# The exponents of seven products of an HGRN2 layer formed on GpSimd instead of VectorE

## The chip, the cores and the metric

One core of a Trainium2 chip runs the whole program. The time is the device time of one execution in microseconds (us). Each engine (TensorE, VectorE, ScalarE, GpSimd, SyncE) works through its own list of instructions in order and waits on semaphores for the others. In the profile TensorE is PE (its weight loads PEld), VectorE is DVE, ScalarE is ACT, GpSimd is POOL and SyncE is SP.

## What is computed

The reference is one step of a two-layer decoder: a retention layer with a dense SwiGLU, then an HGRN2 layer with a top-2-of-8 expert SwiGLU, for one prompt of 256 tokens and 8 single sample tokens. The change touches the HGRN2 layer's recurrence, cut here to what matters:

```python
q = silu(q); forget = lb + (1 - lb) * sigmoid(f)        # 8 heads of 128
k = 1 - forget; logf = log(forget)
# chunks of 64 tokens; b is the running sum of logf in a chunk
b = cumsum(logf)
w = exp(where(t >= s, b[t] - b[s], -inf))
a[t, s] = sum_d q[t, d] * w[t, s, d] * k[s, d]
o = a @ i + (q * exp(b)) @ S
S_new = S * exp(b_last) + (k * exp(b_last - b)).T @ i
```

The sample tokens need one step each: the state of a head (8 samples x 128 x 128) is read from memory, decayed, given its rank-one term and written back.

## The kernel before, in words

The decay between two tokens depends on the channel, so the products of q and k are made level by level. At level l the tokens are cut into groups of 2m (m = 2^l); the later half carries q times exp(b - middle), the earlier half k times exp(middle - b), and one matrix product then gives the pairs of that group. There are ten products, p = 0 to 9: p 0 is the diagonal, p 1 the weighted k for the final state (transposes), p 2 crosses the two blocks of 128 tokens, and p 3 to 9 are the levels 0 to 6.

The stage runs over sixteen tiles t (a projection of 128 output columns each, `HG_TILE`: eight of i, eight of the gate g). `HG_STEP` = (0, 1, 2, 3, 5, 6, 8, 9, 10, 11) says after which tile TensorE makes product p. Product p uses the work array `lev[p % 2]`, and makes four passes over engines before TensorE can begin:

- **exponents(p)** (L1550 to L1580, VectorE): waits until TensorE has finished product p - 2, which read the same array, and writes the differences of the running sums `bcum` into `lev[p % 2]`: for the levels 0 to 5 two subtractions of 128x1024 (L1564, L1565), for level 6 two of 128x512 and two copies (L1568, L1569). It raises `lev_sub`.
- **exponential(p)** (L1085, ScalarE): waits on `lev_sub` and takes exp of the whole array in place (L1088).
- **operands(p)** (L1582, VectorE): two multiplications by q and k (L1592, L1593), then raises `lev_x` for TensorE.
- after the product, **choose** (VectorE, L1599) or **take** (ScalarE, L1090) moves the results out of the banks.

The order of the work in one tile t is written out by hand for each engine:

- VectorE (L1649): choose of the product after tile t - 1; exponents for the product after tile t + 1; scaled(t), which reads the tile out of its bank (L1312); the low part of the weights four tiles ahead (`low_part`, L1317), which waits for ScalarE's high part of the same weights; update_head(t - 1) (L1613, L1620), eight instructions on the samples' state; operands for the product after tile t + 1.
- ScalarE (L1122): take; exponential of the same product; the copies of `itr` (L1133, L1135); the high part of the weights four tiles ahead (L965); the decay of head t's state (L1145).
- TensorE (L2207): the tile; `rows_of_i` (L2107), which waits for update_head(t - 2) and for scaled(t - 1); `spread_i`; the product. A tile goes into bank t % 2, which ScalarE's itr copy has to free.
- GpSimd (L888 to L894): it issues the transfers of the samples' state. Three buffers (`hunit`) are filled ahead; then for h = 0 to 7 it waits for update_head(h), issues the store of head h, waits for the store's end and issues the load of head h + 3. After that it issues the router's weights and three rows of gains (L896 to L903).

So the tiles 2, 4, 5, 7, 8, 9 and 10 form exponents, for the products 3 to 9. The stage's tail follows without exponents, then the output projection, the router and the eight experts, whose weights come from memory one piece after another (SyncE, L788).

Of the kernel before, what the change touches and what calls it, by code (L numbers as in the profile page):

```python
# [7 lines left out]
ALU = mybir.AluOpType  # L8
# [7 lines left out]
P = 128  # L16
# [7 lines left out]
HH = 8  # L24
# [6 lines left out]
CHUNK = 64  # L31
# [126 lines left out]
HG_LEVEL = (None, 8, 7, 0, 1, 2, 3, 4, 5, 6)  # L158
HG_TILE = [("hi", i) for i in range(8)] + [("hg", i) for i in range(8)]
HUNITS = 3  # L160


def products_after(t):

    return [p for p in range(len(HG_STEP)) if HG_STEP[p] == t]
# [111 lines left out]
def hybrid_step(nc, ins, outs):  # L277
    FILL, BANKS = fills()
    with ExitStack() as ctx:
# [63 lines left out]
        def part(tensor, a, *shape):  # L343
            n = int(np.prod(shape))
            v = tensor[:, a:a + n]
            if len(shape) == 2:
                return v.rearrange("p (a b) -> p a b", a=shape[0])
            if len(shape) == 3:
                return v.rearrange("p (a b c) -> p a b c", a=shape[0], b=shape[1])
            return v  # L350
# [60 lines left out]
        bcum = part(arena, 8448, 8, NP_)  # L411
# [3 lines left out]
        lev = [part(ring, scratch + 2048 * j, 2048) for j in range(2)]  # L415
        hs_out = part(ring, scratch, 8, P)

        hunit = [part(ring, a, NS, P) for a in (scratch + 4096, scratch + 5120, spare)]
# [4 lines left out]
        std8 = arena[0:8, 13568:13568 + NT]  # L423
        rstd8 = arena[0:8, 13568 + NT:13568 + 2 * NT]
        oH = hk
        fsmp = part(small, 64, 8, 8)
        tots = part(small, 128, 4, 8)

# [122 lines left out]
        lev_sub = sem("level_exponents")  # L551
# [5 lines left out]
        hu_out = [sem(f"hunit_stored{j}") for j in range(HUNITS)]  # L557
# [36 lines left out]
        def filled(eng, name):  # L594

            b, k = FILL[name]
            eng.wait_ge(bank_full[b], k + 1)
# [5 lines left out]
        def freed(eng, name):  # L603

            b, k = FILL[name]
            eng.wait_ge(bank_free[b], k + 1)
# [240 lines left out]
        @block.gpsimd  # L847
        def _(pool):
            nc.gpsimd.memset(ring[:, spare:spare + 1024], 0.0).then_inc(pad_zero, 1)

            def load_state(u):
                b, h = unit_of(u)
                j = u % UNITS
                if u >= UNITS:
                    pool.wait_ge(unit_out[j], 16 * (u // UNITS))
                pool.dma_start(unit[:, j, :].rearrange("p (k e) -> p k e", k=2), ret_in[b, h])\
                    .then_inc(unit_s[j], 16)

            pool.wait_ge(arrived[0], need[dense[0][0]])
            for u in range(UNITS):  # L860
                load_state(u)
            for p_ in range(PAIRS):
                for u in (2 * p_, 2 * p_ + 1):
                    b, h = unit_of(u)
                    freed(pool, ("vb", u))
                    pool.dma_start(ret_out[b, h], unit[:, u % UNITS, :].rearrange("p (k e) -> p k e", k=2))\
                        .then_inc(unit_out[u % UNITS], 16)
                for u in (2 * p_ + 4, 2 * p_ + 5):
                    if UNITS <= u < NS * RH:
                        load_state(u)  # L870

            for h in range(UNITS):
                pool.wait_ge(unit_out[h], 16 * len(range(h, NS * RH, UNITS)))
            pool.wait_ge(s_store, 16 * RH)
            filled(pool, ("sot", RH - 1))
            nc.gpsimd.memset(zeros, 0.0).then_inc(zero_ok, 1)
            pool.wait_ge(zero_ok, 1)
            nz = YROWS // P
            pool.dma_start(y_scr[:, :].rearrange("(t p) d -> p t d", p=P),
                           zeros.to_broadcast([P, nz, D])).then_inc(zero_stored, 16)  # L880

            def load_h(h):
                if h >= HUNITS:
                    pool.wait_ge(hu_out[h % HUNITS], 16 * (h // HUNITS))
                    filled(pool, ("itr", h - HUNITS + 1))
                pool.dma_start(hunit[h % HUNITS], hg_in[h]).then_inc(hu_in[h % HUNITS], 16)

            for h in range(HUNITS):  # L888
                load_h(h)
            for h in range(HH):  # L890
                freed(pool, ("ib", 1, h))
                pool.dma_start(hg_out[h], hunit[h % HUNITS]).then_inc(hu_out[h % HUNITS], 16)
                if h + HUNITS < HH:
                    load_h(h + HUNITS)  # L894

            pool.dma_start(w_rt, ins["moe_router"][0].rearrange("(k p) e -> p k e", p=P)).then_inc(rt_in, 16)  # L896
            pool.dma_start(gfin, ins["final_norm_g"].partition_broadcast(P)).then_inc(rows_in, 16)
            freed(pool, ("lv", 4, 3))
            pool.dma_start(g_row, ins["norm_ffn_g"][1].partition_broadcast(P)).then_inc(rows_in, 16)
            filled(pool, ("hvar", 0))  # L900
            for c in range(4):
                pool.dma_start(g_group[32 * c:32 * c + 32, 0, :],
                               ins["norm_ffn_g"][1][256 * c:256 * c + 256].partition_broadcast(32)).then_inc(rows_in, 16)  # L903
            pool.wait_ge(h_tok_ok, 3)
            pool.wait_ge(rows_ok, 1)
            pool.wait_ge(xe_ok, 1)
            for t in range(3):
                m = P if t < 2 else NS
                for w in range(2):
                    pool.indirect_dma_start(y_scr[:, :], bass.IndirectOffsetOnAxis(ap=rowi[0:m, w, t:t + 1], axis=0),  # L910
                                            h_tok[0:m, t, :], None).then_inc(x_scattered, 16)

            pool.wait_ge(w_seen, 32)
            for t in (2, 0, 1):
                m = P if t < 2 else NS
                for w, dst in enumerate((ya, yb)):
                    pool.indirect_dma_start(dst[0:m, t, :], None, y_scr[:, :],
                                            bass.IndirectOffsetOnAxis(ap=rowi[0:m, w, t:t + 1], axis=0))\
                        .then_inc(ya_in[t], 16)
# [333 lines left out]
        def _(dve):  # L1253
# [280 lines left out]
                    forget(h - 1)  # L1534
            forget(HH - 1)

            bch = bcum.rearrange("p h (c t) -> p h c t", t=CHUNK)
            T = [bch[:, :, c, CHUNK - 1] for c in range(4)]

            def sums():  # L1540
# [9 lines left out]
            def exponents(p):  # L1550

                l = HG_LEVEL[p]
                if p >= 3:
                    filled(dve, (("kt", 3), ("cr", 1))[p - 3] if p < 5 else ("lv", p - 4, 3))
                L = lev[p % 2]
                lc = L.rearrange("p (h c t) -> p h c t", h=8, t=CHUNK)
                tot = lambda a, b: bch[:, :, a:b, CHUNK - 1:CHUNK].to_broadcast([P, 8, b - a, CHUNK])
                if l <= 5:
                    m = 1 << l
                    n = 2048 // (2 * m)  # L1560
                    bv = bcum.rearrange("p h t -> p (h t)").rearrange("p (n t) -> p n t", t=2 * m)
                    lv = L.rearrange("p (n t) -> p n t", t=2 * m)
                    mid = bv[:, :, m - 1:m].to_broadcast([P, n, m])
                    V.tensor_tensor(lv[:, :, m:], bv[:, :, m:], mid, ALU.subtract)  # L1564
                    i = V.tensor_tensor(lv[:, :, 0:m], mid, bv[:, :, 0:m], ALU.subtract)  # L1565
                elif l == 6:
                    for c in (0, 2):
                        V.tensor_tensor(lc[:, :, c:c + 1, :], tot(c, c + 1), bch[:, :, c:c + 1, :], ALU.subtract)  # L1568
                        i = V.tensor_copy(lc[:, :, c + 1, :], bch[:, :, c + 1, :])  # L1569
                elif l == 7:  # L1570
                    link(V.tensor_tensor(lc[:, :, 0:2, :], tot(0, 2), bch[:, :, 0:2, :], ALU.subtract))
                    V.tensor_tensor(lc[:, :, 0, :], lc[:, :, 0, :], tot(1, 2)[:, :, 0, :], ALU.add)
                    V.tensor_copy(lc[:, :, 2, :], bch[:, :, 2, :])
                    i = V.tensor_tensor(lc[:, :, 3, :], bch[:, :, 3, :], tot(2, 3)[:, :, 0, :], ALU.add)
                else:
                    link(V.tensor_tensor(lc, tot(0, 4), bch, ALU.subtract))
                    for c in range(3):
                        i = V.tensor_tensor(lc[:, :, c, :], lc[:, :, c, :],
                                            tots[:, c, :].unsqueeze(2).to_broadcast([P, 8, CHUNK]), ALU.add)
                i.then_inc(lev_sub, 1)  # L1580
# [68 lines left out]
            for t in range(16):  # L1649
                for p in products_after(t - 1):  # L1650
                    if p == 0 or 3 <= p <= 6:
                        choose(max(p - 2, 0))
                for p in products_after(t + 1):
                    if p >= 3:
                        exponents(p)
                kind, i = HG_TILE[t]
                if kind == "hi" and i >= 2:
                    filled(dve, ("ib", 1, i - 2))
# [720 lines left out]
```

## Time and profile before

| | |
|---|---|
| median of 3 runs | 1653.11 us (1652.49 to 1654.35) |
| profiled execution, span of its instructions | 1650.9 us |
| PE busy, share of the span | 1605.4 us, 97% |
| DVE busy | 621.5 us, 38% |
| ACT busy | 421.5 us, 26% |
| POOL busy | 79.3 us, 5% |
| mean granted TensorE clock | 0.982 of full speed |

A row of the timeline gives the start and the duration in us, the engine, the line, the operation with the tile it writes and those it reads, the form and the number of instructions merged; in brackets stands how long the engine had been idle and what released it. The parts of the chain of waits are read in the same way. The profile's own execution gives the durations; the time of a run is some 2 us more than its span.

### The profile page before, as it was taken

The page shows a single profiled execution, that of the slowest core. Times are in us where ns is not written, and L with a number is a line of the kernel's source. Part 1 is how long each engine was busy: PE and PEld are TensorE (multiplying, and loading weights), DVE is VectorE, ACT ScalarE, POOL GpSimd, SP SyncE. Part 2 cuts the span into 40 slices and gives each one's busy share as a digit, 9 for nine tenths or more (in the row PEclk, how much of TensorE's full clock was granted, in tenths as well). Part 3 has the DMA queues.
Part 4 walks back from the last instruction along what each step waited for, and adds up shares of the span by engine and source line. Part 5 has one row for each costly group of instructions (what it writes and reads, how often), then busy time and mean ns, then how long its engine had stood idle before and what let it go on. Part 6 is the DMA issues. An engine that isn't in the chain of part 4 may idle for free.

```text
span 1650.9 us, 32102 instructions
## 1 busy us (share of the span) xinstructions
PE 1605.4 (97%) x14348; PEld 956.0 (58%) x14348; DVE 621.5 (38%) x934; ACT 421.5 (26%) x606; POOL 79.3 (5%) x106
## 2 busy tenths in 40 slices
PE   7999999999999988999999999999999999999997
PEld 7888877999999988884333333333333333333332
DVE  6666677566656787454010011100101101001114
ACT  4444544444455564632001000000010000100101
POOL 1122221000000011001000000000000000000001
PEclk9999999999999999997999999999999999999999
DMA  9678779455455443356999999999999999999995
GB/s 338 219 268 300 287 258 385 161 170 188 146 186 195 164 140 124 96 227 264 400 412 397 413 417 391 423 418 388 420 401 405 417 386 424 416 392 420 404 408 211
DMA packets 138232, 514.93 MB, mean 312 GB/s; under 512 B 6700, under 2 KB 61172, under 8 KB 129780
## 3 DMA queue, kind: packets, MB, share of 16 engines
q1 hardware_dynamic: 117780, 447.93, 70.1%
q0 software_dynamic: 15824, 57.97, 10.0%
q10 hardware_dynamic: 4496, 7.02, 1.3%
q8 instruction: 113, 1.85, 0.5%
q14 instruction: 19, 0.16, 0.0%
HBM read 472.43 MB, written 40.47 MB: 311 GB/s over the span
## 4 chain that ended last, share of the span: by engine, by line
PE 82%; DVE 8%; issue 2%; DMA 2%; ACT 1%; SPq 0%; POOL 0%; DVEq 0%; ACTq 0%
PE ps L1879 80%; DMA ring<-in_moe_w_down 2%; DVE ring_low_parts L1317 1%; DVE ring L1620 1%; ACT ring_low_parts L965 1%; DVE ring L1366 1%; PE ps L2025 1%; DMA ring<-in_state_retention 1%; DVE arena L1610 1%; DVE ring L1593 0%; DVE ring L1592 0%; DVE ring L1565 0%; DVE arena L1544 0%; DVE ring L1564 0%; DVE expert_arena L1846 0%
## 5 line engine op out<-in xcount | busy, mean ns | idle before, releaser
L1879 PE MATMUL ps<-ring,expert_x_turned 128*32 128x448 f32 x5376 | 508.1, 539 | 0.0
L1879 PEld LDWEIGHTS ps<-ring,expert_x_turned 128*32 128x32 f32 x5376 | 174.5, 110 | 330.9 <-issue 330.9
L1879 PE MATMUL ps<-normed_high,ring_low_parts 128*128 128x264 f32 x1344 | 271.2, 293 | 10.8 <-DVE arena L1312 3.0
L1879 PE MATMUL ps<-ring,expert_hidden_turned 128*32 128x512 f32 x2496 | 269.3, 592 | 0.2 <-DMA ring<-in_moe_w_down 0.2
L1317 DVE TENSOR_TENSOR ring_low_parts<-ring,ring_low_parts 128x1024 fp32r<-128x1024 f32 (+2 forms) x180 | 208.0, 1163 | 97.1 <-ACT ring_low_parts L965 97.0
L965 ACT CAST ring_low_parts<-ring 128x1024 fp32r<-128x1024 f32 (+2 forms) x180 | 180.0, 1001 | 244.4 <-PE ps L1879 240.1
L1879 PEld LDWEIGHTS ps<-normed_high,ring_low_parts 128*128 128x128 f32 x1344 | 220.3, 193 | 13.4 <-ACT arena L1135 3.6
L1811 DVE TENSOR_TENSOR expert_arena<-expert_arena,ps 128x1344 f32<-128x1344 f32 x16 | 24.9, 1554 | 507.2 <-PE ps L1879 507.2
L1879 PEld LDWEIGHTS ps<-ring,expert_hidden_turned 128*32 128x32 f32 x2496 | 81.0, 110 | 186.3 <-issue 184.2
L1879 PE MATMUL ps<-normed_low,ring_low_parts 128*128 128x264 f32 x640 | 163.9, 290 | 0.0
L1879 PE MATMUL ps<-h_parts,ring_low_parts 128*128 128x264 f32 x1056 | 130.0, 285 | 0.2 <-DVE h_parts L1301 0.2
L1879 PEld LDWEIGHTS ps<-h_parts,ring_low_parts 128*128 128x128 f32 x1056 | 129.2, 188 | 0.9 <-DVE h_parts L1301 0.4
L1879 PEld LDWEIGHTS ps<-normed_low,ring_low_parts 128*128 128x128 f32 x640 | 124.3, 194 | 0.3 <-issue 0.2
L1229 ACT ACTIVATE expert_arena<-ps 128x1344 f32<-128x1344 f32 x16 | 20.7, 1291 | 383.6 <-PE ps L1879 383.6
L1220 ACT COPY cst<-ps 32x1536 f32<-32x1536 f32 x16 | 22.9, 1432 | 370.3 <-PE ps L1879 370.1
L1806 DVE TENSOR_TENSOR cst<-ps,cst 32x1536 f32<-32x1536 f32 x16 | 28.0, 1751 | 223.7 <-ACT cst L1220 222.9
L1879 PE MATMUL ps<-mixed_high,ring_low_parts 128*128 128x264 f32 x384 | 76.0, 295 | 1.7 <-DVE normed_high L1684 0.9
L1879 PE MATMUL ps<-expert_piece_slot,expert_x_turned 128*32 128x448 f32 x768 | 75.1, 539 | 0.3 <-DMA expert_piece_slot<-in_moe_w_up 0.3
L1879 PEld LDWEIGHTS ps<-mixed_high,ring_low_parts 128*128 128x128 f32 x384 | 62.2, 194 | 4.7 <-issue 3.4
L1879 PE MATMUL ps<-hidden_high,ring_low_parts 128*128 128x264 f32 x352 | 64.2, 284 | 0.0
L1879 PE MATMUL ps<-ring 128*128 128x128 f32 (+1 forms) x368 | 52.1, 414 | 5.8 <-DVE ring L1593 2.4
L1879 PEld LDWEIGHTS ps<-hidden_high,ring_low_parts 128*128 128x128 f32 x352 | 54.6, 188 | 0.0
(285 smaller groups left out, 1231.3 us busy)
## 6 DMA issues: line engine op xcount, KB each, us to landing
ring<-in_moe_w_gate SPq DMA_DIRECT2D x64, 1792.0 KB, 16.7
ring<-in_moe_w_down SPq DMA_DIRECT2D x48, 2048.0 KB, 21.3
ring<-in_moe_w_up SPq DMA_DIRECT2D x48, 1792.0 KB, 18.4
expert_piece_slot<-in_moe_w_up SPq DMA_DIRECT2D x16, 1792.0 KB, 19.1
ring<-in_ret_w_in SPq DMA_DIRECT2D x8, 2048.0 KB, 12.9
ring<-in_state_retention POOLq DMA_DIRECT2D x32, 512.0 KB, 8.0
out_ret_s<-ring POOLq DMA_DIRECT2D x32, 512.0 KB, 4.8
ring<-in_hg_w_in SPq DMA_DIRECT2D x8, 2048.0 KB, 8.2
```

The costliest lines, as they stand in the source:

```text
L965: A.copy(block_hi(n), block_raw(n)).then_inc(fw_hi_ok, 1)
L1220: A.copy(y_out[64 * q:64 * q + 32], ps[64 * q + 32:64 * q + 64, b:b + TG, :]).then_inc(y_half_ok, 1)
L1229: A.activation(act_g, ps[:, b:b + TG, 0:GW], ACT.Silu).then_inc(gate_ok, 1)
L1317: V.tensor_tensor(block_lo(n), block_raw(n), block_hi(n).bitcast(F32), ALU.subtract).then_inc(fw_lo_ok, 1)
L1366: i = V.scalar_tensor_tensor(out=S, in0=bank(("vb", u)), scalar=ksmp[:, 2 * h + k, b:b + 1], in1=S, op0=ALU.mult, op1=ALU.add)
L1610: i = V.copy_predicated(dst, lvl[:, l - 1, :].unsqueeze(1).to_broadcast([P, 4, P]), src)
L1620: i = V.scalar_tensor_tensor(out=S[:, b, :], in0=bank(("ib", z, h))[:, P * (b % 4):P * (b % 4) + P], scalar=hk[:, h, NP_ + b:NP_ + b + 1], ...
L1806: V.tensor_tensor(y_out[z], ps[z, b:b + TG, :], y_out[z], ALU.add).then_inc(y_ok, 1)
L1811: V.tensor_tensor(act_g, act_g, ps[:, b:b + TG, 0:GW], ALU.mult).then_inc(mult_ok, 1)
L1879: return nc.tensor.matmul(out, lhsT, rhs, start=first, stop=last)
L2025: i = nc.tensor.transpose(bank(("vb", u))[:, P * e:P * e + P], col, ident)
```

## The change

VectorE's `exponents` keeps only the products 1 and 2. The same differences for the products 3 to 9 are formed by a new function of the same name in GpSimd's list, with the same waits for the product that last read the array, and the same signal `lev_sub`. GpSimd's loop over heads becomes a loop over tiles: in tile t it forms the exponents of the product that follows tile t + 1, then issues the load of head t + 1 (for heads 3 to 7), then the store of head t - 1. Before the loop it waits until VectorE's two remaining exponents are done. ScalarE's, TensorE's and SyncE's lists are unchanged, as is the rest of VectorE's.

```diff
+            def exponents(p):
+                G = nc.gpsimd
+                l = HG_LEVEL[p]
+                filled(pool, (("kt", 3), ("cr", 1))[p - 3] if p < 5 else ("lv", p - 4, 3))
+                L = lev[p % 2]
+                if l <= 5:
...
+                    G.tensor_tensor(lv[:, :, m:], bv[:, :, m:], mid, ALU.subtract)
+                    i = G.tensor_tensor(lv[:, :, 0:m], mid, bv[:, :, 0:m], ALU.subtract)
+                else:
...
+                    for c in (0, 2):
+                        total = bch[:, :, c:c + 1, CHUNK - 1:CHUNK].to_broadcast([P, 8, 1, CHUNK])
+                        G.tensor_tensor(lc[:, :, c:c + 1, :], total, bch[:, :, c:c + 1, :], ALU.subtract)
+                        i = G.tensor_copy(lc[:, :, c + 1, :], bch[:, :, c + 1, :])
+                i.then_inc(lev_sub, 1)
             for h in range(HUNITS):
                 load_h(h)
-            for h in range(HH):
-                freed(pool, ("ib", 1, h))
-                pool.dma_start(hg_out[h], hunit[h % HUNITS]).then_inc(hu_out[h % HUNITS], 16)
-                if h + HUNITS < HH:
-                    load_h(h + HUNITS)
+            pool.wait_ge(lev_sub, 2)
+            for t in range(16):
+                for p in products_after(t + 1):
+                    if p >= 3:
+                        exponents(p)
+                if HUNITS <= t + 1 < HH:
+                    load_h(t + 1)
+                if 1 <= t <= HH:
+                    freed(pool, ("ib", 1, t - 1))
+                    pool.dma_start(hg_out[t - 1], hunit[(t - 1) % HUNITS]).then_inc(hu_out[(t - 1) % HUNITS], 16)
...
 @block.vector, in the loop over t
-                for p in products_after(t + 1):
-                    if p >= 3:
-                        exponents(p)
```

## Rows read from the trace of the kernel before

**Rows 1.** Busy time by stage: window, length, then each engine's busy time, clock, DMA
```profile
577.00:679.00 102.00, 90.84 (x700) 88.00 (x698) 81.41 (x140) 56.36 (x131) 13.50 (x16) 0.92 0.40 122
679.00:708.00 29.00, 28.98 (x227) 26.33 (x228) 10.98 (x17) 16.88 (x26) 2.02 (x4) 1.00 0.27 95
790.00:1618.00 828.00, 827.47 (x8446) 274.67 (x8442) 102.47 (x57) 40.90 (x31) 0.00 (x0) 1.00 1.01 407
```

**Rows 2.** Who waited for whom, 577 to 679: total us, times, longest us
```profile
ACT ring L1088 <- DVE ring L1565: 37.6, 6, 10.3
...
DVE ring_low_parts L1317 <- ACT ring_low_parts L965: 20.6, 8, 2.9
```

**Rows 3.** Timeline of DVE through tile 5
```profile
617.73 1.22 DVE L1564 TENSOR_TENSOR ring<-arena 128x1024 f32<-128x1024 f32 x1
618.86 1.22 DVE L1565 TENSOR_TENSOR ring<-arena 128x1024 f32<-128x1024 f32 x1
...
623.33 1.23 DVE L1317 TENSOR_TENSOR ring_low_parts<-ring,ring_low_parts 128x1024 fp32r<-128x1024 f32 x1 [2.91 <-ACT ring_low_parts L965]
624.48 2.15 DVE L1620 SCALAR_TENSOR_TENSOR ring<-ps,arena,ring 128x128 f32<-128x128 f32 x8
```

**Rows 4.** Timeline of ACT: the exponentials, one cast and one take
```profile
591.00 1.91 ACT L1088 ACTIVATE ring<-ring 128x2048 f32<-128x2048 f32 x1 [3.19 <-DVE ring L1565]
...
609.03 1.91 ACT L1088 ACTIVATE ring<-ring 128x2048 f32<-128x2048 f32 x1 [5.75 <-DVE ring L1565]
...
620.11 1.91 ACT L1088 ACTIVATE ring<-ring 128x2048 f32<-128x2048 f32 x1 [5.56 <-DVE ring L1565]
...
622.24 1.06 ACT L965 CAST ring_low_parts<-ring 128x1024 fp32r<-128x1024 f32 x1
...
639.65 1.91 ACT L1088 ACTIVATE ring<-ring 128x2048 f32<-128x2048 f32 x1 [7.26 <-DVE ring L1565]
...
650.73 1.91 ACT L1088 ACTIVATE ring<-ring 128x2048 f32<-128x2048 f32 x1 [5.56 <-DVE ring L1565]
...
664.23 1.91 ACT L1088 ACTIVATE ring<-ring 128x2048 f32<-128x2048 f32 x1 [10.31 <-DVE ring L1565]
...
667.04 3.47 ACT L1111 COPY arena<-ps 16x64 f32<-16x64 f32 x16
```

**Rows 5.** Timeline of POOL: its compute instructions and what follows one
```profile
0.26 0.10 POOL L2370 MEMSET const-float32-0.0<- 128x1 f32 x1 [0.26 <-issue]
...
247.62 0.95 POOL L876 MEMSET ring<- 128x1024 f32 x1 [3.91 <-DMA out_ret_s<-ring]
248.87 1.31 POOL L879 DMA_DIRECT2D y_scr<-ring  x1 [0.30 <-POOL ring L876]
```

**Rows 6.** Timeline of POOL: issues of the head states, stores and one load
```profile
589.00 0.89 POOL L892 DMA_DIRECT2D out_hg_s<-ring  x1 [336.19 <-DVE ring L1620]
...
597.81 0.89 POOL L892 DMA_DIRECT2D out_hg_s<-ring  x1 [3.83 <-DVE ring L1620]
606.19 0.88 POOL L886 DMA_DIRECT2D ring<-in_state_hgrn  x1 [7.49 <-DMA out_hg_s<-ring]
...
616.04 0.89 POOL L892 DMA_DIRECT2D out_hg_s<-ring  x1 [2.56 <-DVE ring L1620]
...
635.32 0.89 POOL L892 DMA_DIRECT2D out_hg_s<-ring  x1 [2.98 <-DVE ring L1620]
646.47 0.89 POOL L892 DMA_DIRECT2D out_hg_s<-ring  x1 [10.26 <-DVE ring L1620]
657.87 0.89 POOL L892 DMA_DIRECT2D out_hg_s<-ring  x1 [10.51 <-DVE ring L1620]
```

**Rows 7.** Timeline of PE: tile 5 after a gap, the products 8 and 9
```profile
611.32 0.39 PE L1879 MATMUL ps<-normed_high,ring_low_parts 128*128 128x264 f32 x1 [1.53 <-ACT arena L1135]
...
670.73 3.84 PE L1879 MATMUL ps<-ring 128*128 128x128 f32 x32 [0.87 <-DVE ring L1593]
...
679.02 3.84 PE L1879 MATMUL ps<-ring 128*128 128x128 f32 x32 [1.54 <-DVE ring L1593]
```

More of the change, by code:

```diff
@@ L425, in hybrid_step @@
         oH = hk
+        bch = bcum.rearrange("p h (c t) -> p h c t", t=CHUNK)
         fsmp = part(small, 64, 8, 8)
@@ L886, in load_h @@
                 pool.dma_start(hunit[h % HUNITS], hg_in[h]).then_inc(hu_in[h % HUNITS], 16)
+            def exponents(p):
[4 more added lines that the diff above has]
+                if l <= 5:
+                    m = 1 << l
+                    n = 2048 // (2 * m)
+                    bv = bcum.rearrange("p h t -> p (h t)").rearrange("p (n t) -> p n t", t=2 * m)
+                    lv = L.rearrange("p (n t) -> p n t", t=2 * m)
+                    mid = bv[:, :, m - 1:m].to_broadcast([P, n, m])
+                    G.tensor_tensor(lv[:, :, m:], bv[:, :, m:], mid, ALU.subtract)
+                    i = G.tensor_tensor(lv[:, :, 0:m], mid, bv[:, :, 0:m], ALU.subtract)
+                else:
+                    lc = L.rearrange("p (h c t) -> p h c t", h=8, t=CHUNK)
+                    for c in (0, 2):
[3 more added lines that the diff above has]
+                i.then_inc(lev_sub, 1)
             for h in range(HUNITS):
                 load_h(h)
-            for h in range(HH):
-                freed(pool, ("ib", 1, h))
-                pool.dma_start(hg_out[h], hunit[h % HUNITS]).then_inc(hu_out[h % HUNITS], 16)
-                if h + HUNITS < HH:
-                    load_h(h + HUNITS)
+            pool.wait_ge(lev_sub, 2)
[8 more added lines that the diff above has]
+                    pool.dma_start(hg_out[t - 1], hunit[(t - 1) % HUNITS]).then_inc(hu_out[(t - 1) % HUNITS], 16)
             pool.dma_start(w_rt, ins["moe_router"][0].rearrange("(k p) e -> p k e", p=P)).then_inc(rt_in, 16)
@@ L1535, in _ @@
             forget(HH - 1)
-            bch = bcum.rearrange("p h (c t) -> p h c t", t=CHUNK)
             T = [bch[:, :, c, CHUNK - 1] for c in range(4)]
@@ L1552, in exponents @@
                 l = HG_LEVEL[p]
-                if p >= 3:
-                    filled(dve, (("kt", 3), ("cr", 1))[p - 3] if p < 5 else ("lv", p - 4, 3))
                 L = lev[p % 2]
@@ L1557, in exponents @@
                 tot = lambda a, b: bch[:, :, a:b, CHUNK - 1:CHUNK].to_broadcast([P, 8, b - a, CHUNK])
[L1558 to L1570, printed above, removed]
+                if l == 7:
                     link(V.tensor_tensor(lc[:, :, 0:2, :], tot(0, 2), bch[:, :, 0:2, :], ALU.subtract))
@@ L1652, in _ @@
                         choose(max(p - 2, 0))
-                for p in products_after(t + 1):
-                    if p >= 3:
-                        exponents(p)
                 kind, i = HG_TILE[t]
```

## The prediction, made before the change was run

> **What bounds the kernel now.** I read the busy time by stage first, then the waits of the stage that the change touches, then the timeline of each of its engines. Over the whole span PE is the busiest, and in the expert part it is busy 827.47 of 828 us beside a saturated memory [rows 1]. Nothing of the change reaches that far, so only a shift of its start can come through. The stage of the levels, 577 to 679, is different: PE shows 90.84 of 102 us with a granted clock of 0.92, DVE 81.41, ACT 56.36, POOL 13.50 [rows 1]. No engine is full; the time is set by a loop that goes from engine to engine. From 679 to 708 PE is full again (28.98 of 29) [rows 1]. So what the stage gains or loses by 679 goes to the end one to one.
>
> The loop is seen in tile 5 [rows 3, 4]. DVE forms exponents from 617.73 to 620.09; ACT, idle for 5.56 us, starts the exponential at 620.11; behind it in ACT's list stand the itr copies and the cast of weights, which starts at 622.24. DVE's low part waits for that cast, idle for 2.91 us, and starts at 623.33; the update of the head follows at 624.48 and ends near 626.5. Then come the operands, and the next tile's exponents. The two waits of that kind sum to 37.6 us of ACT (6 times) and 20.6 us of DVE (8 times) [rows 2]. The reader is to see that **the exponents are on this loop, and that DVE is idle right after them**: a busy engine's work is not saved if the loop still has to wait for the same result.
>
> **The change part by part.**
>
> *What DVE loses.* Six levels of two instructions, each taking its engine 1.13 us from start to start (617.73 to 618.86) [rows 3], and a seventh level, about 1.9: some 15.5 us. In tiles 2, 4, 5, 7, 8, 9 and 10 DVE then comes to the low part earlier and waits there for ACT's cast, which waits behind the exponential. This is a gain only if the exponents come earlier than before.
>
> *What POOL's instruction costs.* The trace has no two-input instruction on POOL. The nearest rows are a memset of the same width, 0.95 us, and one of a single column, 0.10 [rows 5]: 0.85 for one pass over 1024 columns. A subtraction makes three passes, two reads and a write. If all overlap it takes 0.95, if the reads are in series 1.8, if nothing overlaps 2.65 (2.85 with three whole memsets). I take 2.2, the middle of 1.8 and 2.65, since one engine serving three streams is nearer to these than to a fill. From a memset's end to what waited for it on the same queue lie 0.30 us [rows 5]; I add it once a level for ACT's start, against 0.02 from DVE. So a level costs 2 x 2.2 + 0.3 = **4.7 us**, DVE's 2.27; bounds 1.9 and 5.7. Strided blocks of one and two columns (levels 0 and 1) might cost POOL more; no row shows it.
>
> The Trainium skill (GPSIMD Engine Reference, § 3.1) gives 4497 ns for a subtraction-like instruction of 2048 fp32 on GpSimd and 2293 on VectorE. An estimate from that page is 2.25 for each of ours, 4.8 a level, and the sum below would become about 0.6 us larger.
>
> *Where it stands in POOL's queue.* In tile t the exponents stand behind the store of head t - 2, which waits for update_head(t - 2), done by DVE in its tile t - 1. The store's issue takes 0.89 [rows 6] and begins some 0.4 after the update. So they aren't formed as soon as the array is free: they begin 1.3 us after the update, where DVE began after its operands (2.27, in the tiles that have them) and its choose (2.45, likewise). "A level ahead" is at most that lead. Tile by tile, with the shift carried on from store to store [rows 6] and compared with the start of ACT's exponential [rows 4]:
>
> - p 3, tile 2 (before: neither operands nor choose between): 589.00 + 0.89 + 4.7 = 594.6 against 591.00, **+3.6**.
> - p 4, tile 4: the queue also holds the load of head 4, which waits for the end of the store of head 1. That store is issued at 597.81 and its end releases the load at 606.19, 8.4 later, as it runs beside a weight piece of 2 MB. Now: 597.81 + 3.6 = 601.4, + 8.4 = 609.8, load 0.88, store of head 2 0.89, exponents 4.7 = 616.3 against 609.03, **+7.3**. Without the slow transfer it would be + 4.6.
> - p 5, tile 5: 616.04 + 7.3 + 0.89 + 4.7 = 628.9 against 620.11, **+8.8**.
> - p 6, tile 7: 635.32 + 8.8 + 5.6 = 649.7 against 639.65, **+10.1**.
> - p 7, tile 8: 646.47 + 10.1 + 5.6 = 662.2 against 650.73, **+11.5**.
> - p 8, tile 9: 657.87 + 11.5 + 5.6 = 675.0 against 664.23, **+10.8**: here DVE had both operands and choose in front, and POOL wins 0.7.
> - p 9, tile 10: POOL has no store in front and is done near 678.6. ACT first does the exponential of p 8 and the cast (3.2 from 675.0, by 620.11 to 622.24 + 1.06) and the take, 3.47 [rows 4], to 681.7. Exponential (1.9), cast (1.0), low part (1.2) and operands (2.3) follow, ready near 688.1. But PE starts product 8 at 670.73 + 10.8 = 681.5 and needs it and tile 11, 6.75 us (670.73 to 679.02 less the gap of 1.54) [rows 7], so it reaches product 9 at 688.2 and finds it ready; before it was 679.02. **+9.2** at the entry of the full stretch.
>
> *Clock.* After the gap of 1.53 us before tile 5 [rows 7] the matmuls show 0.42 us instead of 0.28, and the stage's mean is 0.92, which is 16 us in 102 at the 1.2 GHz level. The gaps of PE in front of tiles 3, 5, 6, 8 and 9 become some 3 to 5 us long, since the tile's bank is freed by ACT behind the exponential. PE has slack in these very tiles, so I put this at +1, bounds 0 and +3.
>
> *The moved loads.* Each load of heads 3 to 7 is still behind the store that frees its buffer, and now behind the exponents too. ACT's decay of such a head comes after an exponential that waits for the same queue, so the transfer runs beside that wait: 0, bounds 0 and +2. The router's and gain rows' issues come 20 us later, and are needed after 715: 0. POOL's wait for DVE's first two exponents ends before 572: 0.
>
> **Sum.** 9.2 + 1 = +10.2 us on a profiled span of 1650.9, so 1661.1; the median of the runs is 1653.1, some 2.2 above the span, and the forecast for it is **1663.2**.
>
> The sum falls or rises by about 1.25 us for each 0.1 us of POOL's instruction (two to a level, on the loop a little over six times). With 1.8 it is +5, with 2.85 +18.
>
> **The rivals.**
>
> *Faster.* If POOL took less than about 1.4 us for a 128x1024 subtraction, a level would be below what DVE's operands, choose and exponents took together in tiles 5, 7, 8 and 9, and the loop would shorten; at 0.95, the memset's price, the sum is 10.2 - 1.25 x 12.5 = -5, or 1648. For it speaks only that this is the one compute row of POOL at that width; against it that a memset reads nothing. Point of decision: 1.4 us.
>
> *POOL and DVE block each other.* The Trainium skill (SBUF, § Who interferes with whom) says that a VectorE instruction with two SBUF inputs and a GpSimd instruction that reads SBUF exclude each other, the later one waiting for the whole of the earlier. No row of before can show it. As a mechanism here: in tiles 5, 8 and 9 POOL is ready 1.3 us after the update, while DVE's operands (two SBUF inputs) run for 2.27, so POOL waits 1.0 each time, and in tile 10 its last pieces collide with the low part and the operands of product 8 for another 0.5. Sum +3.5 on the forecast, 1666.7.
>
> *POOL is dearer than three passes.* With the small blocks of the low levels at 3.3 us an instruction, a level costs 6.9; 1.1 x 12.5 = +14 on the forecast, about 1677.
>
> *It does not show.* The chain is shorter than worked out (POOL at 1.6, no slow store): within 3.3 us of before.
>
> **How the numbers follow.** Chances: forecast with POOL between 1.8 and 2.7 us and no blocking 0.45; with blocking 0.25; dearer POOL 0.13; no difference 0.09; faster 0.08. The forecast's own range is 1658 to 1670. For 8 in 10 I take 1656.5 to 1674, which leaves out the faster case, most of the same one and half of the dearer one. A measurement of this kernel tells some 0.2% (3.3 us) from no change; slower by more 0.82, within 0.10, faster by more 0.08.
>
> **What would show it.** In the profile after: POOL's L-lines of the subtractions at 2.2 us; ACT's waits for the exponential released by POOL instead of DVE, and growing from the 37.6 us of its six longest to over 50; DVE's wait for the cast growing from 2.9 to between 5 and 8 us in those tiles, with its busy time down by 15.5; PE's gaps in front of tiles 3, 5, 6, 8, 9; the full stretch starting near 688 and everything behind it shifted alike. The steps go wrong if POOL's instruction is short, if the store of head 1 ends early (then -2.7), or if ACT's exponential starts at 594.6, 616, 629, 650, 662 and 675 in no such order.

## The result and the profile after

The changed kernel takes **1661.38 us** (median of 4 runs, 1658.44 to 1664.01) beside 1652.8 us for the kernel before in the same comparison: a ratio of 1.0056, with a 95% interval of 1.004 to 1.0071. It is slower by about 9 us. The prediction was 1663.2 us in a range of 1656.5 to 1674.

| | before | after |
|---|---|---|
| span of the profiled execution | 1650.9 us | 1662.2 us |
| DVE busy | 621.5 us | 608.6 us |
| POOL busy | 79.3 us | 111.2 us |
| stage of the levels (see below) | 112.05 us | 123.60 us |
| from there to the end | 965.3 us | 964.1 us |

The stage is measured from PE's product 0 to its head outputs, both of which stand in the timeline as one row. The two rows of each kernel, before first, then after:

```profile
573.57 3.81 PE L1879 MATMUL ps<-arena 128*128 128x128 f32 x32 [0.20 <-issue]
...
685.62 5.52 PE L1879 MATMUL ps<-arena 128*128 128x128 f32 x48
```

```profile
574.52 3.81 PE L1889 MATMUL ps<-arena 128*128 128x128 f32 x32 [1.75 <-issue]
...
698.12 5.52 PE L1889 MATMUL ps<-arena 128*128 128x128 f32 x48
```

685.62 - 573.57 = 112.05 and 698.12 - 574.52 = 123.60: +11.55 us in the stage. After has 0.95 more in front of it and 1.2 less behind it, which makes the span's 11.3. So the loss is in this stage, and it goes to the end one to one.

The busy time of these two windows, before and then after (columns as in rows 1):

```profile
573.57:685.62 112.05, 100.87 (x785) 98.03 (x786) 83.70 (x142) 63.32 (x139) 13.50 (x16) 0.92 0.45 142
```

```profile
574.52:698.12 123.60, 106.06 (x785) 102.97 (x786) 70.66 (x126) 63.13 (x139) 45.19 (x32) 0.89 0.39 121
```

DVE does 13 us less, in a stage that is 11.5 us longer. Its freed time has become waiting. The waits of after from 577 to 690, which answer to [rows 2]:

```profile
ACT ring L1116 <- POOL ring L902: 45.8, 6, 9.3
DVE ring_low_parts L1345 <- ACT ring_low_parts L993: 39.7, 8, 8.0
```

ACT's wait for the exponents was 37.6 us and is now 45.8, released by POOL; DVE's wait for the cast has grown from 20.6 to 39.7 us, at most 8.0 instead of 2.9. (The window is 113 us long and that of [rows 2] 102, as the stage is longer.) One turn of the loop in after, from the timelines of DVE (L1633 update, L1605 and L1606 operands, L1345 low part), POOL (L922 store, L901 and L902 exponents) and ACT (L1116 exponential, L993 cast), for product 5; it answers to [rows 3, 4]:

```profile
620.06 2.15 DVE L1633 SCALAR_TENSOR_TENSOR ring<-ps,arena,ring 128x128 f32<-128x128 f32 x8
622.13 1.21 DVE L1605 TENSOR_TENSOR ring<-ring,arena 128x1024 f32<-128x1024 f32 x1
623.26 1.22 DVE L1606 TENSOR_TENSOR ring<-ring,arena 128x1024 f32<-128x1024 f32 x1
...
631.80 1.23 DVE L1345 TENSOR_TENSOR ring_low_parts<-ring,ring_low_parts 128x1024 fp32r<-128x1024 f32 x1 [6.97 <-ACT ring_low_parts L993]
```

```profile
622.71 0.91 POOL L922 DMA_DIRECT2D out_hg_s<-ring  x1 [5.11 <-DVE ring L1633]
623.63 3.06 POOL L901 TENSOR_TENSOR ring<-arena 128x1024 f32<-128x1024 f32 x1
626.66 1.88 POOL L902 TENSOR_TENSOR ring<-arena 128x1024 f32<-128x1024 f32 x1
```

```profile
628.58 1.91 ACT L1116 ACTIVATE ring<-ring 128x2048 f32<-128x2048 f32 x1 [7.35 <-POOL ring L902]
...
630.71 1.06 ACT L993 CAST ring_low_parts<-ring 128x1024 fp32r<-128x1024 f32 x1
```

The array of product 5 had been free since product 3, whose matmuls run from 605.55 to 611.31; POOL comes to it at 623.63 because its queue first holds the store that waits for DVE's update (620.06 + 2.15). The exponents end at 628.54, ACT starts at 628.58, the cast follows at 630.71 and DVE's low part at 631.80, after an idle time of 6.97 us. The update behind it, at 632.94, is what POOL's next store waits for: the loop is closed.

### The profile page after: what moved, and what is told of

It is laid out like the page before. It is cut to its first block, busy times and chain, and to the rows that moved or that the text cites. A ratio compares the mean times of both kernels' runs of the same rounds, so it can differ in the third digit from the quotient of the medians.

```text
span 1662.2 us, 32105 instructions
## 1 busy us (share of the span) xinstructions
PE 1603.0 (96%) x14348; PEld 960.8 (58%) x14348; DVE 608.6 (37%) x918; ACT 421.3 (25%) x606; POOL 111.2 (7%) x122
## 4 chain that ended last, share of the span: by engine, by line
PE 78%; DMA 7%; DVE 6%; issue 2%; POOL 2%; ACT 1%; SPq 0%; DVEq 0%; ACTq 0%; POOLq 0%
PE ps L1889 76%; DMA ring<-in_moe_w_down 5%; DVE ring_low_parts L1345 1%; DVE ring L1633 1%; DVE ring L1394 1%; PE ps L2035 1%; ACT ring_low_parts L993 1%; POOL ring L902 1%; POOL ring L901 1%; DMA ring<-in_state_retention 1%; DMA out_hg_s<-ring 0%; POOL out_hg_s L922 0%; DVE arena L1571 0%; DVE ring L1606 0%; DVE ring L1605 0%
## 5 line engine op out<-in xcount | busy, mean ns | idle before, releaser
L1345 DVE TENSOR_TENSOR ring_low_parts<-ring,ring_low_parts 128x1024 fp32r<-128x1024 f32 (+2 forms) x180 | 208.6, 1167 | 116.8 <-ACT ring_low_parts L993 116.7
L993 ACT CAST ring_low_parts<-ring 128x1024 fp32r<-128x1024 f32 (+2 forms) x180 | 180.0, 1001 | 247.0 <-PE ps L1889 242.8
L1889 PE MATMUL ps<-ring 128*128 128x128 f32 (+1 forms) x368 | 55.7, 427 | 6.9 <-DMA ring<-in_state_retention 2.9
L945 POOL DMA_INDIRECT ring<-y_scr,expert_arena x6 | 5.6, 932 | 848.5 <-DMA expert_arena<-in_consts 847.0
```

Of the source, the lines that this page charges most:

```text
L993: A.copy(block_hi(n), block_raw(n)).then_inc(fw_hi_ok, 1)
L1345: V.tensor_tensor(block_lo(n), block_raw(n), block_hi(n).bitcast(F32), ALU.subtract).then_inc(fw_lo_ok, 1)
L1889: return nc.tensor.matmul(out, lhsT, rhs, start=first, stop=last)
```

## The experiments

In each table of results the stage is that of one profiled execution, and its length can differ by up to some 2.5 us between two executions of one kernel (below: 96.7 and 98.4, 100.2 and 97.7). Ratios are to the kernel before on the same chip, with their 95% intervals.

| run | exponents on | order | ratio | interval | stage, us |
|---|---|---|---|---|---|
| before | VectorE | | | | 112.05 |
| after | GpSimd | | 1.0056 | 1.004 to 1.0071 | 123.60 |
| r1 | VectorE | GpSimd's loop over tiles | 1.0014 | 0.9998 to 1.003 | 112.05 |
| r2 | GpSimd | one more subtraction | 1.0088 | 1.0056 to 1.0119 | 129.47 |
| r3 | GpSimd | ahead of the stores | 0.9962 | 0.9942 to 0.9981 | 110.20 |
| r4 | GpSimd | states on SyncE | 0.9933 | 0.9909 to 0.9957 | 104.12 |
| r5 | VectorE | cast first | 0.9919 | 0.9889 to 0.9949 | 96.71 |
| r6 | GpSimd | cast first | 0.9957 | 0.9937 to 0.9977 | 107.13 |
| r7 | GpSimd | ahead, cast first | 0.9933 | 0.991 to 0.9956 | 102.39 |
| r8 | GpSimd | states on SyncE, cast first | 0.9913 | 0.988 to 0.9946 | 100.24 |
| r9 | VectorE | cast first, reads beside | 0.9947 | 0.9921 to 0.9974 | 106.00 |
| r10 | VectorE | cast first, writes beside | 0.9916 | 0.9885 to 0.9946 | 100.19 |
| r11 | VectorE | r5 again | 0.9911 | 0.9884 to 0.9938 | 98.37 |
| r12 | GpSimd | r8 again | 0.9924 | 0.99 to 0.9949 | 97.73 |

**The loop alone (r1).** VectorE keeps the exponents.

```diff
-            for h in range(HH):
...
+            pool.wait_ge(lev_sub, 2)
+            for t in range(16):
+                if HUNITS <= t + 1 < HH:
+                    load_h(t + 1)
+                if 1 <= t <= HH:
+                    freed(pool, ("ib", 1, t - 1))
...
```

> VectorE forms all exponents as before; only GpSimd's loop over tiles is taken from the change, so the loads of heads 3 to 7 keep their place behind the store that frees the buffer, with no exponents in between. Theory (the exponents stand on a loop through the queues, and GpSimd's copy of them is later): the same as before, within 1 us. Rival (the states' loads come too late for ScalarE's decays): most of the 9 us stays, 1658 to 1662.

The stage is 112.05 us, that of before to the hundredth. The runs are 2.3 us longer in the median, where at most 1 was expected, but the interval includes no change. "A tile later" in the code is the same place in the queue; the loss belongs to the exponents.

**One more subtraction (r2).** On the changed kernel, for the levels 0 to 5:

```diff
...
+                    G.tensor_tensor(dump, bv[:, 0:k, m:], mid[:, 0:k, :], ALU.subtract).then_inc(pool_step, 1)
+                    pool.wait_ge(pool_step, p - 2)
                     G.tensor_tensor(lv[:, :, m:], bv[:, :, m:], mid, ALU.subtract)
```

> The changed kernel with one more subtraction of 960 columns on GpSimd in front of those of the levels 0 to 5, written to a place that nobody reads. Each costs some 1.9 us on GpSimd. Theory: the exponents are on the loop, at six places nearly one to one, and the run is 10 to 13 us longer than the changed kernel, 1671 to 1674. Where GpSimd waits for VectorE's operands first the extra one partly runs into the same block, so not less than 8. Rival (the loss is the collisions with VectorE and not the length of the loop): 0 to 4 us more.

The stage grew by 5.9 us over after's, the ratio by 0.0032, some 5 us: between the two expectations (10 to 13 and not less than 8; 0 to 4), so for the whole kernel the theory's was missed. The dose was 1.88 us a level from start to start. Up to ACT's exponential for product 8 it does what the theory says. That starts 685.20 - 575.31 (product 0 in this run) = 109.9 us into the stage, after's 673.76 - 574.52 = 99.2: 10.7 us for six extra instructions. Behind it some comes back. PE's product 8 in r2, then in after:

```profile
691.69 3.84 PE L1893 MATMUL ps<-ring 128*128 128x128 f32 x32 [1.31 <-DVE ring L1610]
```

```profile
682.06 6.79 PE L1889 MATMUL ps<-ring 128*128 128x128 f32 x32 [2.85 <-DVE ring L1606]
```

In r2 VectorE's instructions in front of it did not meet POOL's work (below), which saves 1.8 us beside after, and the product ran at the upper clock level: 3.84 us where after took 6.79. The two make up for the 4.8 us that came back. The lower clock followed on a gap of 2.85 us in after, where r2 has one of 1.31, so it may belong to the order as well. The 10.7 us answer for the loop up to this place only; how much of after's loss is loop and how much is block and clock, r2 does not show alone.

**Exponents ahead of the stores (r3).** The changed kernel with another order in GpSimd's queue and no other edit:

```diff
-            for t in range(16):
...
+            for step in "e3 s0 l3 e4 s1 e5 l4 s2 l5 s3 e6 l6 s4 l7 e7 s5 s6 e8 s7 e9".split():
+                {"e": exponents, "s": store_h, "l": load_h}[step[0]](int(step[1:]))
```

> The changed kernel with another order in GpSimd's queue alone: e3 s0 l3 e4 s1 e5 l4 s2 l5 s3 e6 l6 s4 l7 e7 s5 s6 e8 s7 e9 (e: exponents of a product, s: store, l: load of a head), so that the exponents no longer stand behind the store that waits for VectorE's update. Theory: the same instructions on the same engine are then done before ScalarE asks for them, VectorE's 15.5 us and its waits for the cast go, and TensorE becomes the bound: 9 to 15 us below the kernel before, 1638 to 1644. Rival (GpSimd's price and the block with VectorE cost the time wherever they stand): at or above the kernel before, 1653 to 1660.

The sign is the theory's: with the same instructions on the same engine the kernel is now 0.4% faster than before, and some 0.9% faster than after. The size isn't: 1647.12 us lies between the two expectations. The waits from 577 to 679 name the reason:

```profile
ACT ring L1171 <- DMA ring<-in_state_hgrn: 13.6, 4, 4.9
POOL ring L887 <- DMA out_hg_s<-ring: 12.7, 3, 4.8
ACT ring L1114 <- POOL ring L902: 11.8, 2, 9.3
```

ACT's decays (L1171) had never waited for a state; now four of them do, since the loads of heads 4 to 7 stand behind exponents that wait for a product, at once or with a store between. One queue can't put both first.

**States on SyncE (r4).** The loads and stores leave GpSimd's queue:

```diff
...
+            STATES = {NDENSE - 9: "l0 l1 l2", NDENSE - 3: "s0 l3", NDENSE - 2: "s1 l4 s2 l5 s3 l6 s4 l7 s5", NDENSE - 1: "s6 s7"}
             for n, (name, loads) in enumerate(dense):
+                for step in STATES.get(n, "").split():
+                    {"s": store_h, "l": load_h}[step[0]](int(step[1:]))
...
-            for t in range(16):
...
+            for p in range(3, 10):
+                exponents(p)
```

> The changed kernel with all loads and stores of the head states issued by SyncE, in the order of the kernel before, so that GpSimd's queue holds the exponents alone and each starts when TensorE has finished with its array. Theory (GpSimd's exponents cost time only by what they stand behind; in the reordered run the loads then stood behind them instead, and ScalarE's decays waited 13.6 us): neither wait is left, the stage of the levels is 10 to 15 us shorter than in the kernel before and so is the run, 1637 to 1643. Rival (the block between GpSimd and VectorE keeps what is left): as the reordered run, the stage 2 us shorter.

The decays' wait is down from 13.6 to 1.2 us, the stage at 104.12, 8 us shorter than before (expected 10 to 15, missed by 2); the ratio of 0.9933 (11 us) is inside what was expected. So GpSimd's exponents cost this kernel time by what they stood behind. No run moves the states to SyncE and leaves the exponents on VectorE; but as no decay waited for a state in before, GpSimd's freed queue is the likely source of the gain.

**The cast first, exponents on VectorE (r5).** The kernel before with one edit in ScalarE's list:

```diff
                 for p in products_after(t - 1):
                     take(p)
-                for p in products_after(t + 1):
-                    if p >= 3:
-                        exponential(p)
                 if 1 <= t <= 9:
...
                 ahead((kind, i))
...
+                for p in products_after(t + 1):
+                    if p >= 3:
+                        exponential(p)
                 if t < HH:
```

> The kernel before, exponents on VectorE, with one edit on ScalarE: the exponential comes behind the copies of itr and the cast of weights of its tile instead of ahead of them. Theory: the loop closes over the cast that waits behind the exponential; without that VectorE and TensorE don't wait for it, and the kernel before itself becomes 8 to 14 us shorter, 1639 to 1645, with no work moved to GpSimd. Rival (the loop goes through the array and the operands, and the cast is only beside it): within 3 us of before.

The stage falls to 96.71 us, 15 us below before, with not one instruction less on any engine. The busy time of its stage, and two of its waits from 577 to 679 (the window of [rows 2]):

```profile
575.04:671.75 96.71, 93.20 (x785) 91.66 (x786) 83.69 (x142) 63.42 (x139) 13.51 (x16) 0.98 0.50 161
```

```profile
DVE ring_low_parts L1317 <- ACT ring_low_parts L965: 5.5, 6, 1.6
ACT ring L1088 <- DVE ring L1565: 3.5, 3, 1.2
```

DVE's 83.7 us are those of before, but its wait for the cast is 5.5 instead of 20.6 us and ACT's for the exponents 3.5 instead of 37.6. The exponential had held up the cast, the cast the low part, this the update and the next exponents.

**The cast first in the changed kernel (r6).** The same edit on after.

> The changed kernel, GpSimd's queue as the change has it, with ScalarE's exponential behind the itr copies and the cast of weights of its tile. Theory (the loss of the change is carried by the cast that waits behind the exponential): the stage is 9 to 13 us shorter than in the kernel before, the run 1640 to 1644, although each of the exponents comes as late in its queue as in the changed kernel. Rival (the loss is carried by the operands, which come late too): 1650 to 1660.

Stage 107.13, 16.5 us below after's and 4.9 below before's; the ratio of 0.9957 is 7 us, short of the 9 to 13 in the stage. At 1646.85 us the run lies between what the theory (1640 to 1644) and the rival (1650 to 1660) expected. The theory holds in the main: one edit in ScalarE's list turns the loss into a gain. The rest I put down to the rival's part, since ACT still waits 9.0 us for POOL in four places; no run takes it apart.

**Both edits (r7), and all three (r8).**

> Both edits together on the changed kernel: exponents ahead of the stores in GpSimd's queue, exponential behind the cast in ScalarE's. Theory: TensorE is the bound in the stage, 13 to 16 us shorter than in the kernel before, 1637 to 1640, a little below the kernel before with the cast first (VectorE has 15.5 us less to do). Rival (the loads behind the exponents cost what they cost in the reordered run): 1644 to 1650.

> The states issued by SyncE, the exponents alone on GpSimd, and the cast first on ScalarE. Theory: the stage is bound by TensorE throughout, 15 us shorter than in the kernel before, 1636 to 1639. If it is no shorter than the kernel before with the cast first alone (its stage: 96.7 us), moving exponents to GpSimd buys nothing once the order is mended.

r7 has a stage of 102.39 and 0.9933, r8 100.24 and 0.9913. Both runs are inside what was expected, at 1639.97 and 1637.52 us; neither stage is, with 10 and 12 us below before where 13 to 16 and 15 were expected, and neither is below r5's 96.71. r7 still shows 5.1 us of ACT waiting for states. In r8's timeline of DVE stand operands of 2.98 and 2.91 us where all others are 1.22 to 1.24: the block.

**The block by itself (r9, r10).** On r5, GpSimd works for nobody: ten subtractions in r9, in r10 twenty memsets of the same width.

```diff
...
+                for _ in range(2 if h < 5 else 0):
+                    done += 1
+                    nc.gpsimd.tensor_tensor(dump, bv[:, :, 32:], mid, ALU.subtract).then_inc(pool_step, 1)
+                    pool.wait_ge(pool_step, done)
```

> The kernel before with the cast first, exponents on VectorE, and ten subtractions of 960 columns on GpSimd beside it (two behind the load that follows the stores of heads 0 to 4), whose result nobody reads; it measures the block by itself. If GpSimd's reads and VectorE's instructions with two SBUF inputs exclude each other: VectorE instructions of 1.22 us then show up to 3 us where they meet, GpSimd's of 1.8 up to 3 or 4, and the stage (96.7 us without them) grows by 2 to 8. If they don't: every duration stays at 1.22 and 1.8, and the stage within 0.5 us.

> The control of the run beside it: in the place of each two subtractions four memsets of 960 columns on GpSimd, about the same time of that engine, writing the same place and reading nothing. If it is the reads that block, VectorE's durations stay at 1.22 us and the stage at 96.7, within 0.5; if it is the queue (the later loads and stores behind them), the stage grows as in the run with the subtractions.

The groups of the two kernels, r9 first (all engine time from 575 to 680; the columns are count, busy us, mean ns):

```profile
L1326 DVE TENSOR_TENSOR ring_low_parts<-ring,ring_low_parts 128x1024 fp32r<-128x1024 f32 x13 | 21.1, 1624 | 5.6 <-ACT ring_low_parts L974 5.4
L902 POOL TENSOR_TENSOR ring<-arena 128x960 f32<-128x960 f32 x10 | 25.1, 2505 | 0.6
```

```profile
L1326 DVE TENSOR_TENSOR ring_low_parts<-ring,ring_low_parts 128x1024 fp32r<-128x1024 f32 x13 | 15.9, 1221 | 8.9 <-ACT ring_low_parts L974 8.9
L902 POOL MEMSET ring<- 128x960 f32 x20 | 18.1, 904 | 0.9
```

With reads beside it DVE's low parts take 1624 ns in the mean, single ones up to 3.12 us; with writes 1221 ns, and no DVE instruction of that width is above 1.3 us. POOL's own 960 columns take 1.80 us where nothing meets them (in r2) and 2505 ns here. The durations settle it: GpSimd's reads and VectorE's two-input instructions block one another, in both directions, and GpSimd's writes do not.

The stages are less clean. They are 106.0 and 100.2 us. r10 was expected at 96.7 within 0.5 and missed that: it is 3.5 us above r5 and 1.8 above the second execution of the same kernel (r11 below). In both runs GpSimd's work also delays the loads behind it: ScalarE's decays wait for a state 8.5 us in r9 and 9.2 in r10, and not at all in r5 and r11. So the queue has a part in both, and the 6 us between r9 and r10 are what the blocking of ten useless subtractions costs here, give or take the 2.5 us.

**VectorE or GpSimd in the mended order (r11, r12).** r5 and r8 again, on one chip, in five rounds.

> The kernel before with the cast first, again, beside the next one on one chip. From the stages in the two profiles (96.7 and 100.2 us) it should be 3 us, 0.2%, below the next: ratio to the kernel before 0.990 to 0.992.

> States on SyncE, exponents alone on GpSimd, cast first, again: ratio to the kernel before 0.992 to 0.994 if GpSimd's exponents cost 3 us more than VectorE's in the mended order, below the run beside it if VectorE's 15.5 us had been worth something there.

0.9911 and 0.9924, with intervals that overlap widely, and stages of 98.37 and 97.73 us, the other way round than at first. Both ratios lie in the ranges written down for a difference of 3 us, but the medians are only 1.4 us apart and the stages say the reverse. The 3 us that I had read from one pair of profiles are not confirmed: the two are equal as far as this can tell. The simplest of them, r5, is some 0.8 to 0.9% faster than the kernel before and 1.4% faster than the changed one.

## Why the prediction was right, and where it was off

**The loop.** Right. What was read from [rows 3, 4], that the exponents are on a loop through ACT's cast and that DVE idles behind them, is what r5 takes apart. DVE's 15.5 us (13 measured in the stage) brought nothing. Of the signs, the releaser is POOL as foreseen; ACT's wait is 45.8 us where over 50 was expected, DVE's waits for the cast are 3.0 to 8.0 us where 5 to 8 were, and the entry of the full stretch comes at 691.61 and not near 688.

**The ledger, tile by tile.** Shifts of ACT's exponential against [rows 4], less the 0.95 us that after was late from the start:

| product | predicted | measured |
|---|---|---|
| 3 | +3.6 | 595.02 - 591.00 - 0.95 = +3.1 |
| 4 | +7.3 | 615.70 - 609.03 - 0.95 = +5.7 |
| 5 | +8.8 | 628.58 - 620.11 - 0.95 = +7.5 |
| 6 | +10.1 | 648.73 - 639.65 - 0.95 = +8.1 |
| 7 | +11.5 | 661.28 - 650.73 - 0.95 = +9.6 |
| 8 | +10.8 | 673.76 - 664.23 - 0.95 = +8.6 |
| PE's product 8 | +10.8 | 682.06 - 670.73 - 0.95 = +10.4 |
| PE's product 9 | +9.2 and +1 of clock | 691.61 - 679.02 - 0.95 = +11.6 |

The order and the places are right, with the largest step at products 3 and 4. The slow transfer of the store of head 1 was there again: issued at 601.84, released the load at 610.12, 8.3 us against the 8.4 of [rows 6].

**POOL's instruction.** Mis-sized. In the two instructions that nothing meets, for product 3 in after:

```profile
591.23 1.90 POOL L901 TENSOR_TENSOR ring<-arena 128x1024 f32<-128x1024 f32 x1
593.10 1.90 POOL L902 TENSOR_TENSOR ring<-arena 128x1024 f32<-128x1024 f32 x1
```

1.90 us, 1.87 from start to start, where 2.2 was taken between 0.95 and 2.85. That is twice a memset of the same width (0.95), as if the write ran beside two reads in series; the runs show the time, not the reason. The 0.30 us to the waiter was wrong too: 593.10 + 1.90 = 595.00 and ACT starts at 595.02. A level costs 3.8 us, not 4.7. The blocks of one and two columns (levels 0 and 1) cost nothing extra, but the next ones do, in the first subtraction of a level alone: where no VectorE instruction with two SBUF inputs ran beside it, it took 2.38 us at level 2 (blocks of 4 columns; r3, r4, r7), 2.13 at level 3 (after), 2.04 at level 4 (r3) and 1.96 at level 5 (r2). The second took 1.88 to 1.92 at every level.

The Trainium skill gives 4497 ns for 2048 columns (GPSIMD Engine Reference, § 3.1); the estimate from it was 2.25 for each of ours. The measurement of 1.90 decides.

**The rival of the block.** It was put beside the forecast with 0.25, and it is true; forecast and rival both hold in part, and their errors cancel. The first subtraction of a level takes 3.06, 2.94 and 2.54 us in tiles 5, 8 and 9, where DVE's operands run. Beside the undisturbed 2.38, 2.04 and 1.96 of the same levels that is 0.68, 0.90 and 0.58, some 2.2 us together; the forecast for the rival was 1.0 in each. It was not foreseen for DVE itself. Tile 10 in after, DVE and then POOL:

```profile
676.71 1.77 DVE L1345 TENSOR_TENSOR ring_low_parts<-ring,ring_low_parts 128x1024 fp32r<-128x1024 f32 x1 [3.87 <-ACT ring_low_parts L993]
678.40 1.63 DVE L1605 TENSOR_TENSOR ring<-ring,arena 128x1024 f32<-128x1024 f32 x1
679.96 2.06 DVE L1606 TENSOR_TENSOR ring<-ring,arena 128x1024 f32<-128x1024 f32 x1
```

```profile
676.36 1.04 POOL L907 TENSOR_TENSOR ring<-arena 128x512 f32<-128x512 f32 x1 [2.63 <-PE ps L1889]
677.35 1.61 POOL L908 COPY ring<-arena 128x512 f32<-128x512 f32 x1
678.92 2.01 POOL L907 TENSOR_TENSOR ring<-arena 128x512 f32<-128x512 f32 x1
```

Three DVE instructions of 1.22 us take 5.46, and the level's pieces 1.04, 1.61 and 2.01, where the same forms take 1.04, 0.60 and 1.03 in r2. That is the difference between +8.6 at the exponential and +10.4 at product 8. The length of the wait follows from the rows: it is what was left of the other engine's instruction, less about 0.15 us. In tile 5 DVE's ends at 624.48, 0.85 after POOL's start, and POOL waits 0.68; in tile 8 1.05 (656.45 to 657.50) and 0.90; in tile 9 0.73 and 0.58. The Trainium skill's rule (SBUF — State Buffer, § Who interferes with whom), that the later of the two waits for the whole of the earlier, agrees with these. But it can be more than one instruction. In r3 VectorE, then GpSimd:

```profile
623.86 1.21 DVE L1603 TENSOR_TENSOR ring<-ring,arena 128x1024 f32<-128x1024 f32 x1
624.99 1.22 DVE L1604 TENSOR_TENSOR ring<-ring,arena 128x1024 f32<-128x1024 f32 x1
```

```profile
623.88 4.30 POOL L901 TENSOR_TENSOR ring<-arena 128x1024 f32<-128x1024 f32 x1 [5.35 <-PE ps L1887]
```

GpSimd waited until both were done, though the second started 1.11 us after its own start: 626.21 - 623.88 - 0.15 = 2.18, and 2.13 for a level 3 make 4.31.

**The clock.** Put at +1, bounds 0 and +3; it is nearly the upper bound, all of it in one place. After a gap of 2.85 us product 8 took 6.79 us instead of 3.84. The granted clock of this stretch of after:

```profile
682.00:689.00 7.00, 6.94 (x35) 6.94 (x36) 3.85 (x5) 4.49 (x9) 2.42 (x4) 0.55 0.50 157
```

0.55 of full speed: nearly the whole stretch was at 1.2 GHz, while before had 2.4 at its product 8 (granted clock 1.00 from 670.7 to 677.7). Other low stretches cost nothing: the products 3 and 4 took 5.76 and 5.58 us in after and 3.74 in before, but the next exponentials of ACT waited 8.00 and 7.35 us for POOL. PE's gaps in front of tiles 3, 5, 8 and 9 were 2.94, 0.92, 3.29 and 1.56 us, with none in front of tile 6, where 3 to 5 us were expected in each.

**The sum.** 3.8 instead of 4.7 us a level takes some 5.6 us off at the slope given. The block gives 2.2 on POOL and 1.8 on DVE, the levels 2 to 5 give 0.9, and the clock 2 more than put; together 6.9. The prediction's +10.2 and the measured +11.3 of span and some +9 of the runs lie close because these cancel. The mechanism and the places were read rightly; that the figure is so near is luck.

**The rival "faster" and its point of decision.** It set a price (1.4 us) below which POOL would win. No run has a cheaper POOL, so the price itself is untested. But it took the queue as the change has it: r3 and r4 are faster than before with POOL at 1.9 us. The prediction said that "a level ahead" was no more than a short lead, and stopped there; another order of the queue was worth 13 us of the stage (r3 beside after).

## What to carry to other kernels

Before work is moved off a busy engine, ask what the receiving queue makes it wait for: here six of seven levels stood behind a store that waits for the very engine that was to be relieved. When an engine idles right behind its own work, look one engine further in the loop, and ask which unrelated instruction stands behind the waiting one; here moving the exponential behind the cast in one list was worth 14 to 15 us of the stage (r11, r5), and moving 15 us of work in the mended order nothing that could be measured. TensorE is then busy 93 of the 97 us (r5), so little is left to win; and each two-input instruction of VectorE and each read of GpSimd stop one another. Which of the two weighs more no run shows.

## What the runs showed of the hardware

- A subtraction of 128x1024 fp32 on GpSimd takes 1.90 us alone, and up to 2.38 (first subtraction of level 2, blocks of 4 columns); one of 128x512 takes 1.04 us and a copy of 128x512 0.60 us (r2). A waiter on ScalarE starts 0.02 to 0.04 us after the end (after).
- GpSimd's reads and VectorE's two-input instructions from SBUF stop one another: 1.22 us become up to 3.12 on VectorE (r9), 2.13 become 4.30 on GpSimd (r3), where it waits for two of VectorE's instructions in a row. Twenty memsets on GpSimd changed no VectorE duration (r10).
